# Seven-product chunks of two feed-forward networks: sums of weights made in DRAM by accumulating transfers

## What is computed

```python
def sq_relu_mlp(h, w_up, w_down):
    return jnp.square(jax.nn.relu(h @ w_up)) @ w_down

for layer in range(2):
    h = rms_norm(x, norm_mix_g[layer])
    x = x + (fox_mixer(h, ...) if layer == 0 else mla_mixer(h, ...))
    x = x + sq_relu_mlp(rms_norm(x, norm_ffn_g[layer]), ffn_w_up[layer], ffn_w_down[layer])
```

## Time and profile before

| what | value |
|---|---|
| median of 3 runs | 1981.95 us (1981.42 to 1982.11) |
| the profiled execution | 1981.71 us |
| its span, first to last instruction | 1980.0 us |
| PE busy | 1961.3 us, 99% of the span |
| PE's weight loads busy | 1640.2 us, 83% |
| DVE busy | 1341.7 us, 68% |
| ACT busy | 894.3 us, 45% |
| POOL busy | 60.4 us, 3% |
| TensorE's granted clock | 0.999 of full speed |

### The profile page before, as it was taken

How to read it: one execution, slowest core, us unless ns; L and a number is a source line. 1 busy time by engine, 2 the same in 40 slices (tenths; PEclk the granted TensorE clock), 3 DMA queues, 4 the chain that set the end, 5 groups by cost and what they waited for, 6 DMA issues and landing times.

```text
span 1980.0 us, 29280 instructions
## 1 busy us (share of the span) xinstructions
PE 1961.3 (99%) x10404; PEld 1640.2 (83%) x10404; DVE 1341.7 (68%) x2145; ACT 894.3 (45%) x1417; POOL 60.4 (3%) x114
## 2 busy tenths in 40 slices
PE   9999999999999999999999999999999999999999
PEld 7777789898987887898988788778888888888888
DVE  6555579687777776797787769574444686563545
ACT  4555554445444554544444443474333544432333
POOL 0000000000110110000001100000000000000000
PEclk9999999999999999999999999999999999999999
DMA  4332243323562114523226513211322412223232
GB/s 158 86 85 85 75 148 129 106 79 98 184 205 78 52 49 157 179 69 106 96 99 214 190 46 104 74 64 65 96 96 98 151 43 85 96 95 105 88 99 91
DMA packets 61292, 209.05 MB, mean 106 GB/s; under 512 B 7160, under 2 KB 10232, under 8 KB 61200
## 3 DMA queue, kind: packets, MB, share of 16 engines
q1 hardware_dynamic: 49920, 168.32, 25.8%
q0 software_dynamic: 10560, 37.28, 6.0%
q10 hardware_dynamic: 720, 2.23, 0.3%
HBM read 205.66 MB, written 2.13 MB: 105 GB/s over the span
## 4 chain that ended last, share of the span: by engine, by line
PE 94%; DVE 4%; ACT 1%; DMA 1%; issue 1%; SPq 0%; DVEq 0%; ACTq 0%
PE bank L893 23%; PE bank L895 23%; PE bank L894 23%; PE bank L1216 4%; PE bank L1218 4%; PE bank L1217 4%; PE bank L1016 1%; PE bank L1091 1%; PE bank L1075 1%; PE bank L998 1%; PE bank L1001 1%; PE bank L1043 1%; PE bank L949 1%; PE bank L951 1%; PE bank L950 1%
## 5 line engine op out<-in xcount | busy, mean ns | idle before, releaser
L893 PE MATMUL bank<-b_hi,w_hi 128*128 128x512 f32 x2060 | 813.0, 395 | 6.6 <-DVE w_lo L2764 4.0
L895 PE MATMUL bank<-b_hi,w_lo 128*128 128x512 f32 x2060 | 802.9, 390 | 0.0
L894 PE MATMUL bank<-b_lo,w_hi 128*128 128x512 f32 x2060 | 802.7, 390 | 0.0
L893 PEld LDWEIGHTS bank<-b_hi,w_hi 128*128 128x128 f32 x2060 | 387.2, 188 | 95.9 <-issue 8.2
L895 PEld LDWEIGHTS bank<-b_hi,w_lo 128*128 128x128 f32 x2060 | 387.0, 188 | 81.0
L894 PEld LDWEIGHTS bank<-b_lo,w_hi 128*128 128x128 f32 x2060 | 387.4, 188 | 80.2 <-issue 2.4
L2764 DVE TENSOR_TENSOR w_lo<-w_raw,w_hi 128x1024 fp32r<-128x1024 f32 (+3 forms) x259 | 306.8, 1185 | 210.2 <-ACT w_hi L1810 209.5
L1810 ACT ACTIVATE w_hi<-w_raw 128x1024 fp32r<-128x1024 f32 (+3 forms) x259 | 265.5, 1025 | 263.3 <-PE bank L895 253.6
L3916 DVE SCALAR_TENSOR_TENSOR arena<-bank,vec,arena 128x511 f32<-128x511 f32 x88 | 65.7, 749 | 85.8 <-ACT arena L2658 80.5
L1216 PE MATMUL bank<-parts,w_hi 128*128 128x256 f32 x384 | 108.7, 283 | 3.3 <-DVE x L3113 3.3
L1218 PE MATMUL bank<-parts,w_lo 128*128 128x256 f32 x384 | 107.9, 281 | 0.0
(11 more groups left out here) (398 smaller groups left out, 2537.9 us busy)
## 6 DMA issues: line engine op xcount, KB each, us to landing
w_raw<-in_wstream SPq DMA_DIRECT2D x253, 512.0 KB, 3.5
arena<-in_ada POOLq DMA_DIRECT2D x48, 512.0 KB, 4.3
plain<-in_wseven SPq DMA_DIRECT2D x24, 512.0 KB, 5.0
early<-in_wseven SPq DMA_DIRECT2D x24, 512.0 KB, 6.8
w_raw<-in_wstream SPq DMA_DIRECT2D x12, 384.0 KB, 3.0
arena<-crow POOLq DMA_DIRECT2D x16, 256.0 KB, 4.8
w_raw<-in_wstream SPq DMA_DIRECT2D x10, 256.0 KB, 2.6
x<-in_xT ACTq DMA_DIRECT2D x4, 512.0 KB, 6.6
```

The source lines that it names most:

```text
L893: nc.tensor.matmul(dst, whi, rhs_hi(k), start=(k == 0), stop=False)
L894: nc.tensor.matmul(dst, whi, rhs_lo(k), start=False, stop=False)
L895: last = nc.tensor.matmul(dst, wlo, rhs_hi(k), start=False, stop=(k == n - 1))
```

## The change

The sums of weights are no longer made by DVE. A new DRAM tensor, `seven_sums`, has for each unit four blocks: A+B, B+C, A+B+C and A+B+C+D. POOL fills it by transfers (`sum_turn`), for two units at a time: a copy of all four blocks (2 MB), then with `accum_op=add` B and C onto the first two blocks (1 MB), the first sum onto the third (0.5 MB), and the third sum onto the fourth (0.5 MB). The four steps are staggered over turns: a turn issues the copy for one couple of units, the first addition for the couple before it, and so on, once all transfers of the last turn have landed. A network has 6 couples and 9 turns. The sums for `ff_a` are made in the first attention, a turn behind each `rows`; those for `ff_b` in one go behind the sixth piece of `ada`, within `ff_a`, ahead of the wait for its third stage.

SP then loads every weight by itself, 28 transfers of 256 KB a chunk from the blocks or from the sums, into a ring of 12 places in `plain` and `early`; it waits once for every four, until the low parts of the four that lay there are made, and ACT waits once for every four. Ahead of a network's first such load SP waits for all of its sums. DVE's `two`, `three` and `four` are gone.

```diff
+        SEVEN_RING = 12
+        GROUP = 4
+        PIECE = (0, None, None, 3, None, None, 2)
+        SUM_AT = (None, 1, 2, None, 0, 3, None)
+        UNITS = QUAD * SEVEN_CHUNKS
+
+        def seven_raw(i):
+            r = i % SEVEN_RING
+            return (plain if r < SEVEN_RING // 2 else early)[:, 2 + r % (SEVEN_RING // 2), :]
...
+        sum_in, SUM_STEP = crow_out, 2
+        SUM_TURNS = UNITS // SUM_STEP + 3
...
+            def load_seven(i):
+
+                if i >= SEVEN_RING and i % GROUP == 0:
+                    sp.wait_ge(seven_lo, seven_count(i - SEVEN_RING + GROUP - 1))
+                n, o = i // SEVEN, i % SEVEN
+                src, at = (seven_rows, PIECE[o]) if PIECE[o] is not None else (sum_rows, SUM_AT[o])
+                sp.dma_start(seven_raw(i), src[n * P:(n + 1) * P, at * T:(at + 1) * T]).then_inc(seven_in[i // GROUP % N_GROUPS], 16)
...
                     if c == 0:
 
                         sp.wait_ge(free, count)
+                        sp.wait_ge(sum_in, sum_count(run))
                     if c < SEVEN_CHUNKS:
-                        for q in range(QUAD):
-                            load_seven(QUAD * seven_chunk(run, c) + q)
+                        end = SEVEN * QUAD
+                        for i in range(end):
+                            load_seven(end * seven_chunk(run, c) + i)
...
+            def sum_turn(run, turn):
+
+                first, n = seven_first(run) // SUM_STEP, UNITS // SUM_STEP
+                pool.wait_ge(sum_in, SUM0[run] + 16 * sum(min(max(turn - back, 0), n) for back in range(4)))
+                for back, (to, src, at) in enumerate(((slice(0, 4 * T), seven_rows, slice(0, 4 * T)),
+                                                      (slice(0, 2 * T), seven_rows, slice(T, 3 * T)),
+                                                      (slice(2 * T, 3 * T), sum_rows, slice(0, T)),
+                                                      (slice(3 * T, 4 * T), sum_rows, slice(2 * T, 3 * T)))):
+                    if 0 <= turn - back < n:
+                        units = slice((first + turn - back) * SUM_STEP * P, (first + turn - back + 1) * SUM_STEP * P)
+                        if back:
+                            pool.dma_start(sum_rows[units, to], src[units, at], accum_op=ALU.add).then_inc(sum_in, 16)
+                        else:
+                            pool.dma_start(sum_rows[units, to], src[units, at]).then_inc(sum_in, 16)
...
+            sum_turn("ff_a", 0)
+            for p in range(2, FOX_PAIRS):
+
+                pool.wait_ge(row_min, 6 * p - 6)
+                rows(p, p % 2)
+                sum_turn("ff_a", p - 1)
+            for turn in range(FOX_PAIRS - 1, SUM_TURNS):
+                sum_turn("ff_a", turn)
...
             condition(0, ADA_A, 1)
+            for turn in range(SUM_TURNS):
+                sum_turn("ff_b", turn)
             pool.wait_ge(seven_mm, MM0 + SEVEN * QUAD * SEVEN_CHUNKS)
             condition_row(0)
...
-                        if i % SEVEN == 0:
-                            four(at // SEVEN)
-                        if i % SEVEN == 2 and i + 5 < end:
-                            two(at // SEVEN + 1)
-                        if i % SEVEN == 4 and i + 3 < end:
-                            three(at // SEVEN + 1)
```

More of the change, by code:

```diff
@@ L373, in program @@
         ff_s = [ar(8), ar(9)]
-        seven_in_to = [b[:, 2:6, :].rearrange("p a t -> p (a t)") for b in (plain, early)]
-        seven_pair = plain[:, 6:8, :].rearrange("p a t -> p (a t)")
-        seven_tmp = [b[:, i, :] for b in (plain, early) for i in (6, 7)]
-        def seven_raw(n, o):
-            first, _, third, second = (seven_in_to[n % 2][:, i * T:(i + 1) * T] for i in range(4))
-            return (first, seven_tmp[1], seven_tmp[2], second, seven_tmp[0], seven_tmp[3], third)[o]
+        SEVEN_RING = 12
+        GROUP = 4
+        N_GROUPS = SEVEN_RING // GROUP
+        PIECE = (0, None, None, 3, None, None, 2)
[4 more added lines that the diff above has]
+            return (plain if r < SEVEN_RING // 2 else early)[:, 2 + r % (SEVEN_RING // 2), :]
         def seven_count(i):
@@ L683, in program, with sum_count @@
         wflat = d["wstream"]
-        def seven_src(n):
-            size = 4 * P * T
-            return d["wseven"][n * size:(n + 1) * size].rearrange("(p c) -> p c", p=P)
+        seven_rows = d["wseven"].rearrange("(r c) -> r c", c=4 * T)
+        sum_rows = nc.dram_tensor("seven_sums", (2 * UNITS * P, 4 * T), F32, kind="Internal").ap()
+        def sum_count(run):
+            return SUM0[run] + 16 * 4 * (UNITS // SUM_STEP)
         block = ctx.enter_context(nc.Block())
@@ L722, in load_run @@
                         load(s, 2 * half + s, (2 * half + s) * (P * PANEL), PANEL)
-            def load_seven(n):
-                if n >= 2:
-                    sp.wait_ge(seven_lo, seven_count(SEVEN * (n - 1) - 1))
-                for h in range(2):
-                    cols = slice(2 * T * h, 2 * T * (h + 1))
-                    sp.dma_start(seven_in_to[n % 2][:, cols], seven_src(n)[:, cols]).then_inc(seven_in[n % 2], 16)
+            def load_seven(i):
[4 more added lines that the diff above has]
+                sp.dma_start(seven_raw(i), src[n * P:(n + 1) * P, at * T:(at + 1) * T]).then_inc(seven_in[i // GROUP % N_GROUPS], 16)
             def load_ffn(run, load_panels, free, count):
@@ L803, in rows @@
                     pool.dma_start(c_row[m][h], crow[bass.ds(2 * p + h, 1), 0, :].to_broadcast([P, T])).then_inc(crow_in[m], 16)
+            def sum_turn(run, turn):
[11 more added lines that the diff above has]
+                            pool.dma_start(sum_rows[units, to], src[units, at]).then_inc(sum_in, 16)
             rows(0, 0)
             rows(1, 1)
-            with pool.Fori(1, FOX_PAIRS // 2) as pp:
-                for m in range(2):
-                    pool.wait_ge(row_min, 12 * pp + (6 * m - 6))
-                    rows(2 * pp + m, m)
+            sum_turn("ff_a", 0)
[5 more added lines that the diff above has]
+                sum_turn("ff_a", turn)
             pool.wait_ge(ctx_lo, FOX_PAIRS)
@@ L2085, in high @@
                 def high(i):
-                    n, o = i // SEVEN, i % SEVEN
-                    if o == 0:
-                        act.wait_ge(seven_in[n % 2], IN0 + 32 * (n // 2 + 1))
-                    elif o in (1, 2, 5):
-                        act.wait_ge(seven_add, ADD0 + 3 * n + {1: 1, 2: 2, 5: 3}[o])
-                    act.activation(w_quarter(w_hi, i), seven_raw(n, o), ACT.Copy).then_inc(seven_hi, 1)
+                    group = i // GROUP
+                    if i % GROUP == 0:
+                        act.wait_ge(seven_in[group % N_GROUPS], IN0 + 16 * GROUP * (group // N_GROUPS + 1))
+                    act.activation(w_quarter(w_hi, i), seven_raw(i), ACT.Copy).then_inc(seven_hi, 1)
                 def square(j):
@@ L3080, in low @@
                     dve.wait_ge(seven_hi, seven_count(i))
[L3081 removed]
+                    dve.tensor_tensor(w_quarter(w_lo, i), seven_raw(i), w_quarter(w_hi, i).bitcast(F32),
                                       ALU.subtract).then_inc(seven_lo, 1)
[L3084 to L3101 removed]
                 def read(i):
@@ L3166, in up_tiles @@
                         else:
-                            n0 = QUAD * seven_chunk(run, c)
-                            two(n0)
-                            low(SEVEN * n0)
-                            low(SEVEN * n0 + 1)
-                            three(n0)
+                            low(SEVEN * QUAD * seven_chunk(run, c))
+                            low(SEVEN * QUAD * seven_chunk(run, c) + 1)
                         if not last:
```

20 lines of the change are left out of this document (4 added, 16 removed).

## The result

The changed kernel took 2018.4 us, median of 4 runs (2016.2 to 2024.5). The kernel before took 1981.9 us on the same chip (4 runs, 1981.4 to 1982.1). The ratio is 1.0189, interval 1.0166 to 1.0213: slower by 1.9%. The prediction was 1976.5 us, its range ended at 2015.0. The profiled execution took 2024.5 us, 6 us above the median of its runs, and its span is 2022.7 us; what follows counts within it, so its losses are some 6 us larger than those of a middle run.

What follows compares the result with a forecast made beforehand. PE, busy 99% of the span, was taken as the bound, with DVE's queue holding it in four stages. 1981.7 - 5.7 (DVE's additions) + 0.3 (sums beside loads) = 1976.3 us profiled, 1976.5 as median; range 1974.8 to 2015.

Steps and rivals of the forecast that it cites:

- DVE's additions go: Seven-product stages: DVE's queue no longer late at the seventh product; 1.42 us in each of four stages, 5.7 us gained.
- SP's loads: Seven-product stages: 7.3 MB a chunk in place of 4.2 MB costs nothing when there is no other traffic.
- Sums of the first network: In the attention: turn 5 may end at 206 us; cost from 0 to 60 us, taken as 0.
- Sums of the second network, late or not: In the first network, POOL's turns before L826 at 525 us: cost from 0 to 126 us, taken as 0.
- The pricing in the middle: Second network's sums: each added byte read twice, nothing else doubled, 37.8 MB against 39 MB left, still in time.
- the sums are late: Rival: POOL still in its turns when the first network's third stage ends, DVE and PE wait; about 2002 us, chance 0.41.
- Sums beside loads: First network's stages: loads land 1.7 times slower beside the sums; 0.3 us of stall in all, upper bound 30 us.
- the first rival: The rival that traffic eats the gain where doubled loads run beside the sums: 1980.7 us, chance 0.17.
- traffic eats the gain: Rival: doubled loads beside the sums cost some 1.5 us a stage in three stages, 1980.7 us; chance 0.17.

Runs made afterwards that it cites:

- the kernel with all small pieces: The changed kernel with copies in rows of 4 KB and all additions in rows of 2 KB, two transfers each where one was: 2002.7 us.
- small ones in places with slack: 4 KB copies and 2 KB additions; against the changed kernel, second network's turns 0-2 behind its stages 1 and 2, 3-5 in second attention, 6-8 behind second network's first stage: 1977.2 us.

## Why the prediction was wrong

*DVE's additions go*: right. Predicted was 1.42 us in each of four stages. Stages 4 and 5 of the changed kernel are 1.4 us shorter each, and without the second sums all four are. PE's wait for x of 0.8 us four times is gone there. The total of that kernel, 1977.7 us, is 1.2 us above the forecast, less than the 1.8 us that it loses again behind the networks. DVE's busy time on the page fell by 49 us and not by 62; its additions by their own durations fell by 61, the rest being starts and ends that lay over each other before.

*SP's loads*: right as it was put. Doubled, with nothing beside them but the first network's sums ahead of it, they cost nothing.

*Sums of the first network*: right in price, 0. A full turn took 28 to 30 us and not under 25, with the DMA engines at 0.92 from 38 to 198 us. Turn 5, which had until 206 us, was over at 189.8; the rows for the last pair went out at 173.1 us, where before they went out at 173.7, and landed by 191 us, before the 210.5 at which they are read. PE was busy 159.70 of 160 us.

*Sums of the second network, late or not*: right. The pricing in the middle, an added byte read twice and a copied one counted once, is what the engines show: additions 88 engine-us for a MB, loads 46 to 49, and copies in 4 KB rows 44 (from 301 to 311 us of the kernel with those alone, 1.65 MB in 45.1%). By that the work was 37.8 MB of a budget of 39, so it was in time by little. The turns were over at about 489 us, 36 us ahead of the 525 of the budget, also because SP's queue got less than it asked for; in the kernel with all small pieces, where SP's queue got more, they were over at 517. The Trainium skill (DMA: Bandwidth & Descriptors, section Latency and other measured facts) let me estimate, from its 214 GB/s, 1.5 counted bytes for a copied one; here the copy is no dearer than a load, and the measurement decides. Its section Rules for kernel authors says that an accumulating transfer reads its destination before it writes it; the trace's factor of 2 for additions agrees. So the rival "the sums are late", to which I gave 0.41, is wrong in its mechanism. No instruction waited for a late sum.

*Sums beside loads*: this is the step that failed. I wrote 0.3 us, with 30 us as the upper bound. Against the kernel without those sums it was 41 us by the medians and 46.8 us by the spans of the profiled executions (2022.7 for 1975.9). Three errors lie in the one number.

First, the factor. I took 1.7 from a panel's landing beside other loads, 5.9 for 3.4 us. There both queues had the same kind of work, plain loads of 512 KB in rows of 4 KB. In the stages SP's rows are 2 KB, those of a copy came in pieces of 64 KB and 2.4 to 2.7 us, and additions take 176 ns for 2 KB or 327 ns for 4 KB where a load takes 84. The landing went from 4.5 us for 1 MB to 13 and 14 us for 256 KB. I had noted under the first rival that 256 KB transfers have rows half as long, and gave it no price.

Second, latency in place of a rate. I asked whether a group lands within 10.4 us of cover. The cover is used up once. After that only the rate counts: from 318 to 346 us a stage asks for 187 GB/s, and SP's queue got 106. I had added up the engines' time over 225 us (it suffices, and by little) and not asked who gets it in the 40 us in which a stage needs it.

Third, the upper bound, the cover missed "once in each of three stages". Its own terms give 3 x (10.4 + 2.5) = 39 us, not 30; that this is near the 41 measured is chance. Two stages were hit, not three, and in them PE stood two and three times, 31.1 us in all, each wait shorter than the 12.9 us of one missed cover. With each wait the granted clock fell for some us, another 10 us in both stages, for which the bound had no term.

The rival "traffic eats the gain" named the right mechanism, with 4.5 us for what took some 40; its 1.5 us a stage were not worked out from any row. The sign for it that I wrote down, ACT waiting for a group in the first network's stages and not in the second's, is what the profile shows.

What the runs show of the cause: the traffic of the second sums (with and without, 2018.4 and 1977.7 us), its place (the same large pieces in the second attention leave all stages whole, 1994.4 us; small ones in places with slack, 1977.2 us) and the sizes of rows on both sides (52.3 to 39.7 us by the copies' pieces; 53.6 to 43.0 us by the loads' rows). The rule by which the engines deal out turns is read from counts in the traces. Rows of both queues start one for one from 326 to 330 us in four kernels, and from 348 to 358 us of the changed kernel (352 of SP beside 332 of POOL). Over 330 to 340 us of the kernel with 2 KB loads and 2 KB additions the records have 807 beside 384, but that stretch isn't full: up to 333 us the counts are equal, then POOL's rows fall from 63 in a us to 8, and SP's rise. The records don't name the engine, so it isn't shown engine by engine. What stays open is why small copies are worth 12.6 us of stage 1 without additions and nothing with them; with them SP's queue gets as little from 318 to 346 us, 3.11 MB for 2.98, and the last turn begins 15 us later. Those kernels and the other variants in the table ran once each, which is enough for differences of 12 us and more, not for those of a few.

## What to carry to other kernels

Before bulk traffic is put beside loads that PE waits for, compare rates in that very stretch: what its loads need (bytes over PE's time for them), and what their queue will get when every row of theirs stands behind a longer or dearer row of the other's; room in the mean over 200 us says nothing. Put the bulk where a load is asked for long ahead of its use, spread over turns that wait for each other, and never ahead of an urgent load in the same queue. The change's idea was sound by 4.8 us (1977.2 for 1981.9); its place and its rows were wrong by 41.

## What the hardware showed that I had not expected

A copy in DRAM whose rows are contiguous on both sides goes in pieces of 64 KB (32 by 16384 numbers in POOL's order), and each holds an engine for 2.4 to 2.7 us. The Trainium skill (DMA: Bandwidth & Descriptors, section Rules for kernel authors) advises transfers of 1 MiB and more; both versions of the copy keep to that (one of 2 MB, or two of 1 MB), and the trace has nothing against it. Inside such a transfer the size of the row was free: for the copy alone a byte cost about the same (42 engine-us for a MB, against 44 in rows of 4 KB), and beside loads that are waited for the 4 KB rows took 12.6 us off stage 1.

An accumulating transfer costs the engines twice a load of the same bytes, 88 engine-us for a MB against 46 to 49.

The granted clock falls behind a stall. In the chain of stage 1 of the changed kernel, PE stood for 9.3 us, began again at 361.1 us at one matmul in 0.21 us, and was back at 0.12 us from 366.5 us on:

```profile
361.66 0.21 PE bank L1246
...
365.92 0.21 PE bank L1245
366.49 0.12 PE bank L1246
```

The granted clock is 0.50 from 361.1 to 366.0 us and 1.00 from 366.5 us on; that is the step between the levels of 1.2 and 2.4 GHz, for 5.4 us. Both stages together have 9.9 us more of busy PE than the same matmuls take in stage 3: of the 41 us that they lose against its pace, a quarter is the clock's.
